# Local attention scores from stacked high and low parts, woven into the projection's matmuls

## The reference, cut to what matters

```
qa = apply_rope(rms_norm(sq), ...); ka = apply_rope(rms_norm(sk), ...)
s  = einsum('bnqhgd,bnkhd->bnhgqk', qc, kb) * 64 ** -0.5   # a chunk of 64 queries, 128 keys: its own chunk and the one before
m  = max(max(s), sink);  p = exp(s - m);  denom = sum(p) + exp(sink - m)
o  = einsum('bnhgqk,bnkhd->bnqhgd', p / denom, vb)
```

## Time and profile before

| | us |
|---|---|
| median of 3 runs (2436.54 to 2442.07) | 2439.66 |
| the profiled execution | 2440.97 |
| its span | 2439.2 |
| PE busy | 2254.3 (92%) |
| DVE / POOL / ACT busy | 1441.6 / 1068.8 / 1006.6 |
| mean granted TensorE clock | 0.95 |

### The profile page before, as it was taken

How to read it: one execution, slowest core, us unless ns; L and a number is a source line. 1 busy time by engine, 2 the same in 40 slices (tenths; PEclk the granted TensorE clock), 3 DMA queues, 4 the chain that set the end, 5 groups by cost and what they waited for, 6 DMA issues and landing times. The chain is left out here.

```text
span 2439.2 us, 32369 instructions
## 1 busy us (share of the span) xinstructions
PE 2254.3 (92%) x10408; PEld 1840.7 (75%) x10408; DVE 1441.6 (59%) x2053; ACT 1006.6 (41%) x1717; POOL 1068.8 (44%) x886
## 2 busy tenths in 40 slices
PE   3899999968899999997699998999999989999999
PEld 3798888956676766765588886888878878888887
DVE  4377677766665555434677768776764464344443
ACT  4355555434555555553433334333333223223221
POOL 1255445533335545553655665666636840002210
PEclk8999999967999999998899999999999999999999
DMA  5123222338656565546444445444457764332463
GB/s 200 40 73 92 73 73 73 77 77 227 196 159 187 181 180 180 157 132 221 154 143 152 161 160 216 155 160 159 147 183 257 277 212 140 104 121 104 164 207 112
DMA packets 290541, 371.20 MB, mean 152 GB/s; under 512 B 26288, under 2 KB 185200, under 8 KB 288624
## 3 DMA queue, kind: packets, MB, share of 16 engines
q1 hardware_dynamic: 290416, 369.60, 47.2%
HBM read 244.59 MB, written 124.93 MB: 151 GB/s over the span
## 5 line engine op out<-in xcount | busy, mean ns | idle before, releaser
L327 PE MATMUL f_bank<-f_t_hi,f_w_hi 128*128 128x512 f32 x896 | 352.0, 393 | 24.3 <-DVE f_w_lo L2029 18.3
L327 PE MATMUL f_bank<-f_w_hi,f_a_hi 128*128 128x512 f32 x896 | 351.0, 392 | 13.5 <-DVE f_y L2069 7.8
L327 PE MATMUL f_bank<-f_t_lo,f_w_hi 128*128 128x512 f32 x896 | 351.0, 392 | 0.0
L327 PE MATMUL f_bank<-f_t_hi,f_w_lo 128*128 128x512 f32 x896 | 350.9, 392 | 0.0
L327 PE MATMUL f_bank<-f_w_lo,f_a_hi 128*128 128x512 f32 x896 | 350.4, 391 | 0.0
L327 PE MATMUL f_bank<-f_w_hi,f_a_lo 128*128 128x512 f32 x896 | 350.1, 391 | 0.0
L1405 POOL TENSOR_TENSOR a_p_lo<-a_prob,a_p_hi 128x512 fp32r<-128x512 f32 (+1 forms) x192 | 225.5, 1181 | 281.0 <-DVE a_p_hi L1523 114.4
L327 PEld LDWEIGHTS f_bank<-f_t_hi,f_w_hi 128*128 128x128 f32 x896 | 169.7, 189 | 62.4 <-DVE f_w_lo L2029 19.6
L2048 DVE TENSOR_TENSOR f_a_lo<-f_a_raw,f_a_hi 128x1024 fp32r<-128x1024 f32 x112 | 161.0, 1438 | 89.1 <-ACT f_a_hi L1975 88.9
L327 PEld LDWEIGHTS f_bank<-f_w_hi,f_a_hi 128*128 128x128 f32 x896 | 169.3, 189 | 50.7 <-issue 13.9
L1937 POOL TENSOR_TENSOR f_r<-f_r,f_y 128x512 f32<-128x512 f32 x24 | 41.6, 1771 | 364.4 <-DMA f_r<-s_x 364.4
(11 more groups left out here) (294 smaller groups left out, 4997.5 us busy)
## 6 DMA issues: line engine op xcount, KB each, us to landing
f_a_raw<-s_aop SPq DMA_DIRECT2D x112, 512.0 KB, 4.3
w_raw<-in_w_ff SPq DMA_DIRECT2D x64, 512.0 KB, 5.2
s_aop<-f_a SPq DMA_DIRECT2D x128, 256.0 KB, 2.7
s_aop<-f_s SPq DMA_DIRECT2D x96, 256.0 KB, 2.3
f_w_raw<-in_w_ff SPq DMA_DIRECT2D x64, 256.0 KB, 5.7
f_t_raw<-s_hop SPq DMA_DIRECT2D x14, 1024.0 KB, 8.3
f_r<-in_w_ff SPq DMA_DIRECT2D x48, 256.0 KB, 5.6
a_vals<-s_v SPq DMA_DIRECT2D x40, 264.0 KB, 4.5
```

What stands on the lines that cost most here:

```text
L327: ins = pe.matmul(out, a, b, start=(first and j == 0), stop=(last and j == n - 1))
```

## The change

The low part of q moves to partitions 64 to 127 of one tile, `q_st`, whose lower half is the high part. `k_hi` gets 128 partitions, and ACT fills the upper 64 with a copy of the lower ones, in two further instructions per tile; the second rounding (L674) is now waited for first, so are six counts on `h_act`. A block of scores is then two matmuls: 128 rows deep (q_hi and q_lo, both against k_hi) and 64 rows deep (q_hi against k_lo). PE waits for `h_act`, too. The last 6 of cut 0's 24 matmuls move in between the blocks (three behind block 0, three behind block 2), and the latent products behind blocks 3 (pB, 128 rows), 5 (pB, 64 rows) and 6 (pC). `scored` is counted at the last block. In steps 16 and 17 there is no cut to move; the latent products are woven in all the same.

```diff
-    H_ACT, H_DVE = 4, 4
+    H_ACT, H_DVE = 6, 4
-        q_hi = sb("q_hi", [SD, 2, SH, CHUNK], F32R)
-        q_lo = sb("q_lo", [SD, 2, SH, CHUNK], F32R)
-        k_hi = [sb(f"k_hi{b}", [SD, SKV, 3, CHUNK], F32R) for b in range(2)]
+        q_st = sb("q_st", [P, 2, SH, CHUNK], F32R)
+        q_hi, q_lo = q_st[0:SD, :, :, :], q_st[SD:, :, :, :]
+        k_hi = [sb(f"k_hi{b}", [P, SKV, 3, CHUNK], F32R) for b in range(2)]
...
-                        st.add(ac.activation(k_hi[t.b][:, :, 0:2, :], src, ACT.Copy))
-                        st.add(ac.activation(k_hi[1 - t.b][:, :, 2, :], src[:, :, 1, :], ACT.Copy))
+                        st.add(ac.activation(k_hi[t.b][0:SD, :, 0:2, :], src, ACT.Copy))
+                        st.link(ac.activation(k_hi[1 - t.b][0:SD, :, 2, :], src[:, :, 1, :], ACT.Copy))
+                        st.add(ac.activation(k_hi[t.b][SD:, :, 0:2, :], k_hi[t.b][0:SD, :, 0:2, :].bitcast(F32), ACT.Copy))
+                        st.add(ac.activation(k_hi[1 - t.b][SD:, :, 2, :], k_hi[1 - t.b][0:SD, :, 2, :].bitcast(F32), ACT.Copy))
...
-                def cut(t, j):
+                def cut(t, j, ks=range(KD)):        # the slices ks of a cut; waits before the first, counts after the last
+                def up(t, k):                       # k = 0, 1: pB from 128 and from 64 rows; k = 2: pC
...
-                        cut(t0, 0)
+                        cut(t0, 0, range(0, 6))
                     t = tile_at(i, s - 2)
                     if live(t, NT):
                         wait(pe, h_dve, (t.n + 1) * H_DVE)
-                        for n in range(2):
-                            for hp in range(HP):
-                                ... ins = products(pe, out, [(*lhs, k_hi[t.b][:, g, pick, :], k_lo[t.b][:, g, pick, :])])
-                        ins.then_inc(scored, 1)
-                        ... products(pe, pB[:, 0:LH * LD], ...); products(pe, pC[:, :], ...)
+                        wait(pe, h_act, (t.n + 1) * H_ACT)
+                        for b in range(NB8):
+                            ...
+                            q = q_st[:, n, 2 * hp:2 * hp + 2, :].rearrange("d h q -> d (h q)")
+                            pe.matmul(out, q, k_hi[t.b][:, g, pick, :], start=True, stop=False)
+                            ins = pe.matmul(out, q[0:SD, :], k_lo[t.b][:, g, pick, :], start=False, stop=True)
+                            if b == NB8 - 1:
+                                ins.then_inc(scored, 1)
+                            if b in (0, 2) and live(t0, NT):
+                                cut(t0, 0, range(6 + b // 2, 7 + b // 2))
+                            if b in (3, 5, 6):
+                                up(t, (3, 5, 6).index(b))
+                    elif live(t0, NT):
+                        cut(t0, 0, range(6, KD))
```

More of the change, by code:

```diff
@@ L808, in body @@
                         src = pB[0:SD, 0:SKV * P].rearrange("d (g n q) -> d g n q", g=SKV, n=2)
-                        st.add(dve.tensor_tensor(k_lo[t.b][:, :, 0:2, :], src, k_hi[t.b][:, :, 0:2, :].bitcast(F32), ALU.subtract))
-                        st.add(dve.tensor_tensor(k_lo[1 - t.b][:, :, 2, :], src[:, :, 1, :], k_hi[1 - t.b][:, :, 2, :].bitcast(F32), ALU.subtract))
+                        st.add(dve.tensor_tensor(k_lo[t.b][:, :, 0:2, :], src, k_hi[t.b][0:SD, :, 0:2, :].bitcast(F32), ALU.subtract))
+                        st.add(dve.tensor_tensor(k_lo[1 - t.b][:, :, 2, :], src[:, :, 1, :], k_hi[1 - t.b][0:SD, :, 2, :].bitcast(F32), ALU.subtract))
                         st.end()
@@ L923, in _ @@
             def _(pe):
-                def cut(t, j):
+                def cut(t, j, ks=range(KD)):
                     a, z = CUTS[j]
                     prior = (t.n - 1) * N_ACT + 4 + 2 * j if j < 2 else t.n * N_ACT + 2
[L928 to L931, removed]
+                    if ks[0] == 0:
+                        wait(pe, n_act, prior)
+                    ins = products(pe, pP[(t.b + j) % 2][:, 0:z - a],
+                                   [(xT_hi[t.b][:, k, :], xT_lo[t.b][:, k, :], W["in_hi"][:, k, a:z], W["in_lo"][:, k, a:z])
+                                    for k in ks], first=ks[0] == 0, last=ks[-1] == KD - 1)
+                    if ks[-1] == KD - 1:
+                        ins.then_inc(projected, 1)
+                def up(t, k):
+                    if first(t) and k == 0:
+                        wait(pe, up_lo, 3)
+                    if k == 2:
+                        products(pe, pC[:, :], [(lat_hi[:, 2, :], lat_lo[:, 2, :], ukv_hi[:, :], ukv_lo[:, :])]).then_inc(up_made, 1)
+                        return
+                    r = (P, LQR - P)[k]
+                    ins = products(pe, pB[:, 0:LH * LD], [(lat_hi[0:r, k, :], lat_lo[0:r, k, :], uq_hi[0:r, k, :], uq_lo[0:r, k, :])],
+                                   first=k == 0, last=k == 1)
+                    if k == 1:
+                        ins.then_inc(up_made, 1)
                 def body(i, s):
@@ new lines, in body @@
+                        for b in range(NB8):
+                            n, hp = b // HP, b % HP
+                            g = hp * 2 // SG
+                            pick = slice(0, 3, 2) if n == 0 else slice(0, 2)
+                            out = pG[:, b * KEYS:(b + 1) * KEYS].rearrange("p (a k) -> p a k", a=2)
+                            q = q_st[:, n, 2 * hp:2 * hp + 2, :].rearrange("d h q -> d (h q)")
[9 more added lines that the diff above has]
+                        cut(t0, 0, range(6, KD))
```

## The result

The changed kernel takes 2444.88 us (median of 9 runs, 2439.3 to 2447.54), the kernel before 2439.29 (9 runs, 2432.9 to 2442.07): a ratio of 1.0026, 95% interval 1.0014 to 1.0037. It is slower by 5.6 us, by more than the measurement's doubt; the forecast was 2450.5 in a range of 2432 to 2466. The profiled execution took 2442.05, with a span of 2440.3.

A forecast was written before the change was run, and what follows sets the result against it. PE was taken to bound the 14 steps, an engine chain the last two tiles. Changes of depth +14 and clock -13.5 made about 0, plus 11 for the tail: 2450.5 us, range 2432 to 2466 (forecast's own 2444 to 2458).

The forecast's parts named there:

- The bound: PE busy 92% of the span and throughout the 14 steps; in the last two tiles a chain through several engines.
- The changes of depth: PE's 128/64-row changes: 16 instead of 4 per tile, 0.16 us each, 1.9 us more per tile at full clock.
- The net of a step: PE per tile at full clock: 1.9 us for changes less 0.9 for matmuls saved, net +1.0; +14 over 14 steps.
- Rivals 1: Changes of depth cost nothing when single instructions alternate: about 2410 us; chance 0.10.
- 2 (half of it, 0.08): Changes of depth cost about half and the tail's `scored` is less late: about 2432 us; chance 0.15.
- The clock: 14 steps: 5 spells at 1.2 GHz in place of 14, 1.5 us each, 13.5 us back.
- rival 3: The clock never falls in the 14 steps: +4, about 2444 us; chance 0.08.
- The waits in a step: Within the 14 steps: `scored` and DVE's chain 3.2 us later, covered by idle time; no PE wait.
- The margin of 4.4 us: DVE's idle 2.53 us before xT_lo plus 1.83 before the next tile's sums, taken to cover the 3.2 us delay.
- ACT's copies: Two further copies on ACT, 0.7 us with their wait, hidden; at worst 0.7 us a tile, 10 in all.
- The drain: Last two tiles: late `scored` costs +6.6 and +4.4 us, together +11, bounds +1 to +12.
- at half clock everything on PE doubles: Second last tile: `scored` 11.7 us behind its first score, where it is 5.1 now: +6.6.

The follow-up runs named there:

- pad_klo: Changed kernel with k_lo zero-padded to 128 partitions, so each block's second pass is 128 rows deep: 2410.34 us, ratio to before 0.9890.
- pad_all: As pad_klo, with pB's second slice also contracted over 128 rows by zeros in the added weights: 2400.8 us, ratio to before 0.9854.
- before_128rows: Kernel before, same order and 24 score matmuls, with q, k and pB's second slice zero-padded to 128 rows: 2405.24 us, ratio 0.9866.
- mix_only: Kernel before with the new order alone, three 64-row passes per block, no stacking, no ACT copies: 2440.79 us, ratio 1.0018.
- stack_only: Changed kernel with the order of before: cut 0 whole, 8 blocks of 128- and 64-row passes, then latent products: 2471.71 us, ratio to before 1.0140.
- pad_ups_last: As pad_all, but latent products behind the last block, only cut 0's six matmuls woven in: 2393.75 us, ratio to before 0.9819.
- after_tail_plain: Changed kernel with latent products behind the last block in steps 16 and 17, which have no projection: 2436.57 us, ratio to before 0.9995.

## Why the prediction was right

*The bound.* It held: PE is busy all through the 14 steps before, and each change on PE came out in the time. After the change it has gaps, but small ones, in the six steps of the loop (below).

*The changes of depth.* The mechanism is shown by pad_klo and pad_all, which keep every matmul, its columns and its place and take only the changes away; by before_128rows, where the four changes of before go; and by mix_only, where six are added. The size I took, 0.16, lies between what the experiments give: 0.13 among single instructions, 0.16 to 0.19 around runs. The net of a step was forecast at +1.0 and is +0.7. Rivals 1 (no cost) and 2 (half of it, 0.08) fell. The loads of the kernel before, at the change to the 64-row half of pB, whose matmuls start at 193.36 and 193.64:

```profile
193.36 0.18 PEld L327 LDWEIGHTS p_pB<-p_uq_hi,p_lat_hi 64*128 64x128 f32 x1 [0.25 <-issue]
193.47 0.19 PEld L327 LDWEIGHTS p_pB<-p_uq_lo,p_lat_hi 64*128 64x128 f32 x1
```

The first load behind the change starts with its own matmul, after 0.25 us in which nothing was loaded; the second, of the same depth, starts 0.17 us ahead of its matmul. The Trainium skill's rule that a change of tiling mode drains the engine ("TensorEngine Tiling (Array Packing)", section Key Properties) agrees with this case: each change costs 0.13 to 0.19 us. Of loads pulled ahead of running matmuls (the Trainium skill, "TensorE: Matmul & The Clock Gate", section "Step-by-step: what each phase is for") this trace shows the 0.17 us within one depth and none across a change.

*The clock.* Here the number was wrong: 5 spells were forecast, none came, as rival 3 had it, and its sum (2444) is nearer to the measured time than the forecast's. mix_only shows that the weaving is enough for this, with the 64-row passes left as they were. I had thought of the changes of depth as time that would bring the clock down. In stack_only, with 18 changes and nothing woven in, it fell in every one of the 14 steps, more than before; in mix_only, with 10, and in the changed kernel, with 16, it never fell. So changes of depth alone do not bring it down; what it is in stack_only that does, no run separates.

*The waits in a step.* The margin of 4.4 us was too kind. The next matmul that depends on DVE's chain is not the next step's score but L1029, which waits for l_lo, and it comes before the second of the two idle times that I had added up. With the delay of the scores (2.92 to 5.64 us of wait) the 2.53 us of idle time before xT_lo are used up, L893 takes 1.06 us in place of 0.23, and the loop's steps pay 0.66 each. The prediction had this term at nothing, and that step of it failed, though the rule behind it, that a late count is free only while the chain behind it has slack, is what pad_ups_last shows.

*ACT's copies.* Forecast as hidden, with 0.7 us for both; at most a small cost, open as said. They take 0.42 and 0.29 us.

*The drain.* +11 was forecast and +8.1 measured. The chain is the one forecast: from the second last tile's first score to L1029 it is 4.5 us more (17.3 to 21.8; forecast +6.6), and from the last tile's first score to its exponential, which now waits for the subtraction, 3.1 us more (8.9 to 12.0; forecast +4.4). The mis-sized term is "at half clock everything on PE doubles": alternating passes start 0.40 us apart there (486.43 to 486.83), not 2 x (0.11 + 0.16) = 0.54, so the maxima came 9.9 us behind the first score in place of 11.9. The matmul's own time doubles, from 0.11 to 0.215 us, but the change on top of it costs 0.19 at half clock and 0.14 at full. after_tail_plain takes 6.3 us of the drain's 8.1 back by the order alone.

The sum was forecast as 0 + 11. In the profiles it came as about -5.5 from 105 us to the start of the last projection and +8 from there on, and in the medians as 5.6. The mechanisms and their signs were right but for the wait; four sizes were not. The clock was put 7.5 us too dear, the changes some 4, the drain 3, and the wait's 4 us were left out, which partly made up for the others. That the time came so near, at the lower edge of the forecast's own 2444 to 2458, is in part luck.

## What to carry to other kernels

Before splitting a contraction into passes of different depth, count how often PE changes between 64 and 128 rows: here each time cost more than a whole narrow matmul, and zeros in the unused partitions made it free. Here a stacked pass paid only when its partner had the same depth: with both, and the old order, the same idea that had cost 5.6 us took 2.0% off, 1.3% of it from depth alone (before_128rows). Where an instruction that others wait for is moved later, look for the first thing on the waiting engine's chain that the bound engine needs, and count the slack only up to there.

## What the runs showed of the hardware

- A matmul of 64 rows and one of 128 rows with the same columns take the same time in a row of their kind, 0.11 us at 128 columns (before and before_128rows). Where the two kinds alternate, the next start comes after 0.25 us at full clock and 0.40 at half.
- The granted clock fell although PE was busy. A run of 24 matmuls of 64 rows and 128 columns was followed by a fall from 2.4 to 1.2 GHz in 10 of 14 steps; the same 24 with 128 rows, half of them zeros, by none in 14 steps. Nor did it fall in the 14 steps where wide matmuls stood between the 64-row ones (mix_only, the changed kernel).
- A DVE operation on four elements per partition (the one that adds kr_sum) took 0.23 us, or as long as POOL's 128x1024 scaling beside it still ran, up to 1.66 us; its mean over the 14 steps rose from 0.74 to 1.09 us with the change. The trace shows this in each of the 28 steps; no experiment moved the one or the other.
